# State-space layer on one core: the part across chunks without its carried product

## What is computed

```python
a_cs   = cumsum(a, axis=-1)                       # inside each chunk
y_diag = einsum('bcgls,bgrcls,bcsgrp->bclgrp', cb, exp(segsum(a)), x)
states = einsum('bclgn,bgrcl,bclgrp->bcgrpn', B, exp(a_cs[..., -1:] - a_cs), x)
y_off  = einsum('bclgn,bcgrpn,bgrcl->bclgrp', C, states_of_chunk_before, exp(a_cs))
y      = y_diag + y_off
```

## Time and profile before

| | |
|---|---|
| median of three runs | 1130.92 us |
| span of the profiled execution, first to last instruction | 1129.8 us |
| PE busy | 1110.7 us (98%) |
| DVE busy | 937.4 us (83%) |
| ACT busy | 705.6 us (62%) |
| POOL busy | 183.3 us (16%) |
| chain of work that ended last | PE 85%, DVE 9%, ACT 4%, issue 1%, DMA 1% |

### The profile page before, as it was taken

How to read it: one execution, slowest core, us unless ns; L and a number is a source line. 1 busy time by engine, 2 the same in 40 slices (tenths; PEclk the granted TensorE clock), 3 DMA queues, 4 the chain that set the end, 5 groups by cost and what they waited for, 6 DMA issues and landing times.

```text
span 1129.8 us, 23543 instructions
## 1 busy us (share of the span) xinstructions
PE 1110.7 (98%) x8902; PEld 1069.8 (95%) x8902; DVE 937.4 (83%) x1656; ACT 705.6 (62%) x1033; POOL 183.3 (16%) x233
## 2 busy tenths in 40 slices
PE   7999999999999999999999999999999999999997
PEld 6999999999998999999999998999998999999987
DVE  5899886788888978877888889789987778988784
ACT  6777785566665457885766654464867357766531
POOL 1000241111112200000111122011224100433310
PEclk9999999999999999999999999999999999999999
DMA  7565447655557864334655569585343754655571
GB/s 273 168 233 193 171 144 255 233 196 182 180 175 281 302 226 179 115 113 147 216 182 180 187 223 324 164 288 187 117 164 122 261 187 150 209 194 185 182 271 38
DMA packets 43711, 220.18 MB, mean 195 GB/s; under 512 B 8063, under 2 KB 12656, under 8 KB 22640
## 3 DMA queue, kind: packets, MB, share of 16 engines
q1 hardware_dynamic: 31552, 185.25, 47.5%
q0 software_dynamic: 9264, 30.94, 7.6%
q10 hardware_dynamic: 2816, 2.90, 0.9%
HBM read 217.97 MB, written 1.11 MB: 194 GB/s over the span
## 4 chain that ended last, share of the span: by engine, by line
PE 85%; DVE 9%; ACT 4%; issue 1%; DMA 1%; POOL 0%; DVEq 0%; ACTq 0%
PE ps L884 65%; PE ps L989 8%; PE ps L993 4%; DVE wl L570 3%; ACT wh L556 2%; DVE work L2534 1%; PE ps_idle L1170 1%; PE ps L1538 1%; DMA work<-running_sums 1%; DVE actr L2376 0%; PE ps_idle L1060 0%; PE ps L1067 0%; DVE work L2339 0%; PE ps L1372 0%; PE ps L1515 0%
## 5 line engine op out<-in xcount | busy, mean ns | idle before, releaser
L570 DVE TENSOR_TENSOR wl<-raw,wh 128x2048 fp32r<-128x2048 f32 x176 | 397.5, 2259 | 56.8 <-ACT wh L556 56.0
L884 PE MATMUL ps<-xh,wl 128*128 128x256 f32 (+1 forms) x1504 | 426.9, 284 | 0.4 <-DVE work L2534 0.2
L884 PE MATMUL ps<-xh,wh 128*128 128x256 f32 (+1 forms) x1504 | 424.5, 282 | 0.0
L884 PE MATMUL ps<-xl,wh 128*128 128x256 f32 (+1 forms) x1504 | 423.0, 281 | 0.0
L556 ACT ACTIVATE wh<-raw 128x2048 fp32r<-128x2048 f32 (+1 forms) x178 | 333.6, 1876 | 91.4 <-PE ps L884 38.5
L884 PE MATMUL ps<-actr,wh 128*128 128x256 f32 (+1 forms) x1640 | 294.2, 281 | 0.0
L884 PEld LDWEIGHTS ps<-xh,wl 128*128 128x128 f32 x1504 | 283.7, 189 | 3.0 <-issue 2.1
L884 PEld LDWEIGHTS ps<-xl,wh 128*128 128x128 f32 x1504 | 284.6, 189 | 0.8 <-issue 0.8
L884 PEld LDWEIGHTS ps<-xh,wh 128*128 128x128 f32 x1504 | 284.7, 189 | 0.0
L884 PEld LDWEIGHTS ps<-actr,wh 128*128 128x128 f32 x1640 | 251.9, 188 | 0.2
L884 PE MATMUL ps<-actr,wl 128*128 128x256 f32 (+1 forms) x820 | 235.4, 287 | 2.4 <-DVE actr L2376 1.7
(11 more groups left out here) (302 smaller groups left out, 1200.9 us busy)
## 6 DMA issues: line engine op xcount, KB each, us to landing
raw<-in_up SPq DMA_DIRECT2D x66, 1024.0 KB, 5.0
ada_w<-in_w_ada POOLq DMA_DIRECT2D x54, 256.0 KB, 5.6
raw<-in_xbc SPq DMA_DIRECT2D x12, 1024.0 KB, 5.5
work<-in_w_ada POOLq DMA_DIRECT2D x42, 256.0 KB, 5.5
raw<-in_z SPq DMA_DIRECT2D x8, 1024.0 KB, 5.1
raw<-in_so SPq DMA_DIRECT2D x8, 1024.0 KB, 5.0
raw<-in_dn0a SPq DMA_DIRECT2D x8, 1024.0 KB, 5.1
raw<-in_dn1a SPq DMA_DIRECT2D x8, 1024.0 KB, 5.8
```

The lines of the kernel that those rows point to most:

```text
L570: nc.vector.tensor_tensor(wl[:, b % RING, 0:n], raw[:, b % RING, 0:n], wh[:, b % RING, 0:n].bitcast(F32), ALU.subtract).then_inc(lo_done, 1)
L884: mm = nc.tensor.matmul(o, l, r, start=start and n == 0, stop=stop and n == 2)
```

## The change

The two factors of `y_off` are applied elsewhere. ACT takes the exponential of the 32 running sums of chunk 1 once (`reach_rows`) and writes them to a small array in DRAM. For each group POOL broadcasts its 8 rows onto all partitions (`chunk_reach`, 512 KB) into `reach`, a single buffer that lies in `ada_w` (unused until later). DVE multiplies them in place by the cross block (`crossed`), at the place in its order where `carried_scaled` stood. `y_by_feature` then multiplies `xdte` by `reach` where it multiplied `yoffs` by the identity. `carried`, `carried_scaled`, their bank and one small matmul of the running sums are gone.

```diff
@@ POOL
+            def chunk_reach(gr):
+                pool.dma_start(reach.rearrange("p h l -> p (h l)"), reach_of_group(gr)).then_inc(reach_in, 16)
             running_sums(0)
             wait_misc(pool, "cb3")
             running_sums(1)
+            pool.wait_ge(reach_out, 16)
+            chunk_reach(0)
             running_sums(2)
             for gr in range(3):
                 wait_misc(pool, f"y{gr}", 1)
+                chunk_reach(gr + 1)
                 for n in range(2 * gr + 3, min(2 * gr + 5, 8)):
                     running_sums(n)
                 y_low(gr)
@@ PE
-                nc.tensor.matmul(ps_dt[:, 224:256], tri[:, 0, :], a_t[:, 1, :], start=True, stop=True)\
-            def carried(gr):
-                g = PL.G[f"yo{gr}"]
-                acquire(pe, g)
-                given_back(pe, PL.G[f"cb{gr}"])
-                pe.wait_ge(xdte_done, gr + 1)
-                nc.tensor.matmul(bank(g), cbm[:, gr, P:T], xdte, start=True, stop=True).then_inc(misc_done, 1)
             def y_by_feature(gr):
-                given_back(pe, PL.G[f"yo{gr}"])
+                pe.wait_ge(xdte_done, gr + 1)
+                pe.wait_ge(cross_done, gr + 1)
-                            nc.tensor.matmul(o[rows, P:T], yoffs[:, 64 * h:64 * h + 64], ident[:, :],
+                            nc.tensor.matmul(o[rows, P:T], xdte[:, 64 * h:64 * h + 64], reach[:, h, :],
...
@@ ACT, after first_tap(7, 0)
-            A(e12, ps_dt[:, 192:256], ACT.Exp).then_inc(e12_done, 1)
+            A(e12, ps_dt[:, 192:224], ACT.Exp).then_inc(e12_done, 1)
+            A(reach_rows[32:64, :], ps_dt[32:64, 64:192], ACT.Exp).then_inc(reach_done, 1)
+            act.wait_ge(reach_done, 1)
+            act.dma_start(reach_t.ap(), reach_rows[32:64, :]).then_inc(reach_out, 16)
@@ ACT, y_square of group 0
                     act.wait_ge(rows_out, 16)
+                    act.wait_ge(reach_out, 16)
@@ DVE
             def x_carried(gr):
                 if gr:
-                    wait_misc(dve, f"yo{gr-1}")
+                    wait_misc(dve, f"y{gr-1}", 1)
-            def carried_scaled(gr):
-                g = PL.G[f"yo{gr}"]
-                wait_misc(dve, f"yo{gr}")
-                if gr:
-                    wait_misc(dve, f"y{gr-1}", 1)
-                give_back(V.tensor_tensor(heads(yoffs), heads(bank(g)), over(e12[:, 32 + 8 * gr:40 + 8 * gr]),
-                                          ALU.mult), g)
+            def crossed(gr):
+                dve.wait_ge(reach_in, 16 * (gr + 1))
+                given_back(dve, PL.G[f"cb{gr}"])
+                m = cbm[:, gr, P:T].rearrange("p (a b) -> p a b", a=1).to_broadcast([P, 8, P])
+                V.tensor_tensor(reach, reach, m, ALU.mult).then_inc(cross_done, 1)
...
```

More of the change, by code:

```diff
@@ L157, in make_plan @@
     pl.tile("xbc8", 1)
-    pl.misc("yo0")
     pl.tile("xbc9", 0)
@@ L171, in make_plan @@
     pl.tile("za1", 0)
-    pl.misc("yo1")
     pl.close("gns0")
@@ L181, in make_plan @@
     pl.tile("za2", 1)
-    pl.misc("yo2")
     pl.close("gns1")
@@ L190, in make_plan @@
     pl.close("gns2")
-    pl.misc("yo3")
     pl.tile("za3", 1)
@@ L458, in build_program @@
         csb_in, e12_done = [sem(f"csb_in{b}") for b in range(3)], sem("e12_done")
+        reach_done, reach_out, reach_in, cross_done = sem("reach_done"), sem("reach_out"), sem("reach_in"), sem("cross_done")
         grms_done, skip_done = sem("grms_done"), sem("skip_done")
@@ L596, in build_program @@
         xdte = W(6 * KB, 512)
-        yoffs = W(23 * KB, 512)
         zs = W(13 * KB, 4, T)
@@ L600, in build_program @@
         xdt = W(19 * KB, 2, 512)
-        cs_rows = W(12 * KB, P)
+        cs_rows, reach_rows = W(12 * KB, P), W(12 * KB + P, P)
+        reach = ada_w[:, :, :].rearrange("p a n -> p (a n)").rearrange("p (h l) -> p h l", l=P)
         def csb(gr, c):
@@ L671, in build_program @@
         dt_t, a_t = S(2, 32), S(2, 32)
-        e12, ea = S(64), S(32)
+        e12, ea = S(32), S(32)
         lam2, lam4, negl, sgs = S(2), S(2), S(1), S(1)
@@ L698, in build_program, with reach_of_group @@
         sums_t = nc.dram_tensor("running_sums", (64, P), F32, kind="Internal")
+        reach_t = nc.dram_tensor("reach_rows", (32, P), F32, kind="Internal")
+        def reach_of_group(gr):
+            return bass.AP(reach_t, 8 * P * gr, [[0, P], [1, 8 * P]])
         def sums_of_group(gr, c):
@@ L1150, in running_sum_matmuls @@
                 nc.tensor.matmul(ps_dt[0:64, 64:192], a_all, tri[:, 0, :], start=True, stop=True)
-                nc.tensor.matmul(ps_dt[:, 192:224], later[:, :], a_t[:, 0, :], start=True, stop=True)
-                nc.tensor.matmul(ps_dt[:, 224:256], tri[:, 0, :], a_t[:, 1, :], start=True, stop=True)\
+                nc.tensor.matmul(ps_dt[:, 192:224], later[:, :], a_t[:, 0, :], start=True, stop=True)\
                     .then_inc(cs_sums, 1)
@@ L1256, in _ @@
             slab_tile("xbc8", 1)
-            carried(0)
             slab_tile("xbc9", 0)
@@ L1270, in _ @@
             slab_tile("za1", 0)
-            carried(1)
             group_sums(0)
@@ L1280, in _ @@
             slab_tile("za2", 1)
-            carried(2)
             group_sums(1)
@@ L1289, in _ @@
             group_sums(2)
-            carried(3)
             slab_tile("za3", 1)
@@ L2668, in _ @@
             split_lo(dve, PL.S["xbc11"])
-            carried_scaled(0)
+            crossed(0)
             decays(0, 0)
@@ L2694, in _ @@
             group_inverse(0)
-            carried_scaled(1)
+            crossed(1)
             split_lo(dve, PL.S["za2"])
@@ L2718, in _ @@
             decays(2, 1)
-            carried_scaled(2)
+            crossed(2)
             split_lo(dve, PL.S["zb3"])
@@ L2739, in _ @@
             x_dt(3, 1)
-            carried_scaled(3)
+            crossed(3)
             split_lo(dve, PL.S["so"] + 0)
```

## The result

The changed kernel takes 1133.78 us (median of 20 runs, 1131.58 to 1137.28), the kernel before 1130.94 (20 runs, 1129.57 to 1135.57). The ratio is 1.0027, 95% interval 1.0019 to 1.0034: about 3 us more, small but beyond what the measurement leaves open. The forecast was 1131.1 and no measurable change, with a range up to 1133.7: wrong, and just outside. Run again beside other kernels (change_again), the change measured 1133.87, ratio 1.0034 (1.0020 to 1.0048). One execution of fill_wait (1342.7 us), one of sums_first (1906.8) and one of the kernel before (3820.6) are left out of what follows.

The account below looks back on a forecast made before the run. PE bounds the stage up to 130 us, POOL's broadcasts for a moment around 131.8. Sum: 1129.8+1.1, less 4x0.86, plus 3x0.86, 0.55 and 0.53, one half-clock stretch as before: 1131.1 us; range 1127.8 to 1133.7.

Parts of the forecast that it names:

- one stretch at half clock as before: PE near 150 or instead at 134: one half-rate stretch costing 1.7 us, 1.1 of it hidden if at 134.
- two such stretches: Clock-alone rival: two half-rate stretches give 1131.7, none 1130.5; both inside the forecast's own range, no separate chance.
- y(0): Group 0: PE arrives 0.86 earlier at 92.83, decay products are seen at 93.1, so 0.3 us is lost.
- rs5: Group 2: running-sums broadcast 5, behind the decay broadcast on POOL's queue, lands at about 132.3, +0.55 us.
- DVE's added 0.53 per group: DVE: a 1.23 us product replaces a 0.69 scaling in each group, 0.53 longer; bounds 0 and 0.76.
- the two terms: Before y(2): rs5 later by 0.55 plus the new product's 0.53 make y(2) late by 1.08 us.
- rs7: Group 3: running-sums broadcast 7, issued 1.08 later behind the decay broadcast, moves segments(3,1) to about 153.0, +2.5 us.
- From 165 us on: After the stage: PE works without a gap and carries the shift to the end one for one.
- What lies outside the span: Whole run: 1.1 us laid around the span of 1129.8 to reach the three runs' median of 1130.92.
- Edits costed at nothing: Terms at zero: x_carried's wait, fewer PSUM bank takes, the half-wide exponential; ACT's added 0.9 us and small matmul also uncounted.
- the slower one: Broadcasts at 125 land together, rs5 at 134.15, with two half-clock stretches: +2.8, 1133.7 us; chance 0.19.
- Rival 1: Faster: broadcasts don't queue or start earlier, rs5 is there when DVE asks; 1126.3 to 1128.0 us, chance 0.19.

Follow-up runs that it names:

- fill_wait: The changed kernel with six idle matmuls of 128x256 in PE's wait before group_sums(1); 1134.30 us, ratio 1.0019.
- sums_first: The changed kernel with POOL's order turned round in each group, running sums ahead of the decay broadcast; 1130.22 us, ratio 0.9992.
- second profile: Profile of the changed kernel as it is, from its run again beside other kernels; span 1131.0 us, stage begins at 60.23.
- before_plus_broadcasts: The kernel before, carried products kept, with the exponential, row write and four decay broadcasts added, rows unread; 1132.72 us, ratio 1.0020.
- first profile: Profile of the changed kernel from its first measurement; span 1133.1 us, about 1.6 of its 3.3 us over before already there when the stage begins.
- early_issue: The changed kernel with POOL handing out loads as soon as it sees y(1) and y(2), ahead of products that stood before them; 1128.61 us, ratio 0.9976.
- before_early_issue: The kernel before with POOL handing out running_sums(5), (6) and (7) in the same early places, no decay rows; 1129.80 us, ratio 0.9993.
- fill_small: The changed kernel with six idle matmuls before group_sums(1) and five in the first tile of up2; 1131.67 us, ratio 0.9998.
- before_and_fill: The kernel before with two idle matmuls before each contraction step of the first tile of up2; 1134.58 us, ratio 1.0035.

## Why the prediction was wrong

The step that failed is the clock's, the last term of the sum: "one stretch at half clock as before", worth 1.7 us in either place and, at the new wait, hidden for 1.1 us in the wait for y(2). Even two such stretches were put at 1131.7 only. The stretch at the new wait was twice as long and came on top. Measured: 3.45 us between 130 and 145 in both profiles, and in the second profile the 1.65 near 155 beside it, not in its stead. In the second profile DVE's product for y(2) ended at 140.51 (139.29+1.22), but y(2) began at 142.62, because PE was late itself. At full rate its sums (1.92) and its tile (24 matmuls, 2.95 in the row at 219.71) would have ended at 134.94+1.92+2.95 = 139.8. So 2.8 us were lost there, 0.7 of them hidden in the wait for DVE and 2.1 not. The text had taken 1.7, 1.1 of them hidden.

The other steps, by the second profile:

- y(0) at 93.45 after a wait of 0.45 for the decay products (forecast 93.1 after 0.3): right, a little low.
- POOL's issues at 124.79 (124.65), rs5 at 132.63 (132.3): right in kind, in order and one behind the other. rs5 is 0.9 later than before, not 0.55. The group sums begin at 134.94, +0.88 and not +0.54.
- DVE's added 0.53 per group: right. From rs5 to the end of the product for y(2) it took 0.52 longer than before to the end of the old scaling (139.10), so +1.41 there, against 1.08 from the two terms.
- rs7: segments(3,1) at 155.58, +5.1 and not +2.5. Most of the excess is y(2)'s 3.3 instead of 1.08, passed on by POOL, which hands out the loads 3.3 later than before. In the second profile y(3) then begins 2.3 us later than before and in the first it waits 0.97 us for decays(3,1); forecast was +0.2 and no wait.
- From 165 us on PE was to work without a gap and to carry the shift to the end one for one. The kernel before has waits of PE there (1.70 us at 933.44, and 1.3 and 0.8 between 500 and 920), and the shift does not reach the end whole: DVE's instructions in the second profile are 2.5 us later than before up to 875 us and 1.3 from 912 on. The reason stays open.
- What lies outside the span: 1.98 us (median of the runs) in the kernels with the change, 1.75 in those that keep the carried product, before_plus_broadcasts among them; the text had taken one figure for both, 1.1, which is the distance of one span to the median of other executions. The change adds 0.2 us here.

Edits costed at nothing were rightly so: ACT's exponential and write (its wait of 1.36 before the next work is left), the decay rows (no wait in any group), x_carried.

Of the rivals, the slower one named 1133.7 and had its time almost to the tenth, but half by another way. Its loads would have landed together after 133.5; they landed in order, with rs5 at 132.63 (133.51 in the first profile, whose stage begins 1.6 later). Its second half, a stretch at half rate at the new wait as well as the one at 150, is what the second profile shows. So its number was in part luck. The chance of 0.19 was too low because the clock was tied to that landing, when the forecast's own wait of 3 us was enough. Rival 1 needed rs5 in time, and early_issue comes near it: with rs5 there 1.2 us after DVE asks, 1128.6, where the rival had 1126.3 to 1128.0.

On the rule that the prediction weighed (the Trainium skill, TensorE: Matmul & The Clock Gate, section "Why this matters for your kernels": idle gaps between bursts bring the clock back to half rate): the trace now speaks for it at this place. Six idle matmuls in the gap, nothing else changed in fill_wait, and the stretch is at 1.00 instead of 0.77. By that rule the sum was to rise by at most 0.6; its direction was right and the price put on it was not. The gaps here, 2.52 and 2.66 us, are shorter than those that the page's row names. Nor is a gap all that decides: sums_first waited 1.17 us at this place and had a stretch of 3.4 us at half rate from 136.3, before_plus_broadcasts waited 1.63 and kept its clock.

What stays open: why the second place, at 931 to 936 us, falls in some executions and not in others, of kernels that keep the carried product too (before_early_issue at 933.1; by their clocks, 0.992 to 0.999, also executions of the kernel before). The profiled execution of the kernel before has the same wait of 1.70 us there and no fall. The place was seen and filled, its cause was not tried.

## What to carry to other kernels

A load that is already late at its consumer must get nothing in front of it in its queue; look instead what the issuing engine does before the issue, here two products whose results nobody needed yet, and the same change turns from a loss of 0.3% into a gain of 0.24%. When a change adds a wait on TensorE, price the wait and, as a term of its own, the work behind it at half rate; lay that against what follows on TensorE, not against another engine's wait. A few idle matmuls in such a wait kept the clock here; they must fit in it by their measured duration.

## What was not expected of the hardware

- Every half-rate stretch seen between 130 and 1000 us begins near sums of one column: from 0.6 us before the start to 1.2 us behind the end of the group sums of groups 1 and 2, and 0.6 to 2.2 us ahead of the last norm's, behind a wait of PE of 1.7 us. That at 151.2 in the kernel before had the sums alone, without a wait ahead. The group sums near 112 and 170 us have none in any profile.
- One POOL product of 128x256 took 2.79 us in the change before the issues and 0.73 in early_issue. Both rows are of POOL's timeline, first the change, then early_issue:

```profile
123.07 2.79 POOL L832 TENSOR_TENSOR actr<-work,actr 128x256 fp32r<-128x256 f32 x1
```

```profile
119.64 0.73 POOL L832 TENSOR_TENSOR actr<-work,actr 128x256 fp32r<-128x256 f32 x1
```

- An idle matmul of 128x256 (ident and tri) stands as two records whose starts lie 0.215 us apart, 0.43 for one (six fill the time from 132.05 in fill_small), where a tile's matmul of the same size is one record every 0.12. Two of them ahead of a product, in before_and_fill, held it back by 0.68 to 0.71 us only, as it starts 0.03 us behind their last record.
